# Head 0 of a hybrid trunk layer: recurrent input loaded and convolved during the input projection, loads from two queues, no barrier, an own place for the last modulation row

## The reference, cut to what matters

```python
sh1, sc1, g1, sh2, sc2, g2 = jnp.split(mod, 6, axis=-1)      # mod = silu(c) @ w_mod + b_mod
proj = h @ lp['w_in']
xr, gr, q, k, v, gates = jnp.split(proj, SPLITS, axis=-1)    # 1024, 1024, 1024, 1024, 1024, 4096 columns
xc = centred_conv(xr, lp['conv_w'], lp['conv_b'])            # 4 taps along the tokens
y, h_fin = rglru_bidir(xc, wr, br, wi, bi, lam, h0)          # r, i = sigmoid(block_diag(xc, w)); two scans
out_a = (y * jax.nn.gelu(gr)) @ lp['w_a_out']
q, k = apply_rope(q), apply_rope(k)                          # latent tokens only
o = diff_attn(q, [ctx_k, k], [ctx_v, v], lam)                # two softmax maps a head, 8 heads of 128 columns
out_b = rmsnorm(o) @ lp['w_b_out']
out = (sigmoid(ga) * out_a + sigmoid(gb) * out_b) @ lp['w_o']
```

## Time and profile before

| | us |
|---|---|
| median of 3 runs | 2991.76 |
| lowest and highest run | 2989.57, 2995.67 |
| profiled execution, span | 2987.8 |
| TensorE busy | 2856.4 |
| VectorE busy | 2190.0 |
| ScalarE busy | 1555.4 |
| GpSimd busy | 285.9 |

### The profile page before, as it was taken

One profiled execution on the slowest core, in us unless ns is written; L12 is line 12 of the kernel. 1 busy time (PEld: TensorE's weight loads), 2 busy tenths in 40 slices (PEclk: granted clock), 3 DMA queues, 4 the chain that ended last, 5 costly groups with the idle time before them and its releaser, 6 DMA issues.

```text
span 2987.8 us, 42700 instructions
## 1 busy us (share of the span) xinstructions
PE 2856.4 (96%) x15690; PEld 2306.2 (77%) x15690; DVE 2190.0 (73%) x1948; ACT 1555.4 (52%) x1510; POOL 285.9 (10%) x350
## 2 busy tenths in 40 slices
PE   7999999999899999999999995999999999999994
PEld 3589999998899999989998773666666666666662
DVE  7639688795677777763344467888888888888886
ACT  7721212224455555552232444777777777777774
POOL 1000000002111111100000000000000001101100
PEclk9999999999999999999999997999999999999997
DMA  9668677683333333354443655999999999999996
GB/s 378 243 210 257 203 251 238 212 267 100 105 118 118 118 118 118 118 185 139 119 134 130 243 207 218 357 387 390 377 396 382 388 385 385 377 380 381 391 385 239
DMA packets 292924, 757.58 MB, mean 254 GB/s; under 512 B 20329, under 2 KB 184721, under 8 KB 228193
## 3 DMA queue, kind: packets, MB, share of 16 engines
q1 hardware_dynamic: 266640, 638.47, 59.0%
q0 software_dynamic: 23664, 102.29, 10.6%
q10 hardware_dynamic: 2544, 15.82, 1.3%
HBM read 700.61 MB, written 55.89 MB: 253 GB/s over the span
## 4 chain that ended last, share of the span: by engine, by line
PE 79%; DVE 10%; issue 4%; DMA 4%; ACT 3%; DVEq 0%; SPq 0%; POOL 0%; ACTq 0%; POOLq 0%
PE ps L480 16%; PE ps L481 15%; PE ps L482 15%; PE ps L2039 7%; PE ps L2041 7%; PE ps L2040 7%; DVE mod_acc L1386 4%; PE ps L2175 2%; PE ps L2174 2%; PE ps L2176 2%; PE ps L1943 2%; PE ps L2102 1%; DMA raw<-in_w_mod 1%; DVE probs L1602 1%; DVE w_lo L435 1%
## 5 line engine op out<-in xcount | busy, mean ns | idle before, releaser
L413 DVE TENSOR_TENSOR we_lo<-raw,we_hi 128x2048 fp32r<-128x2048 f32 x384 | 876.4, 2290 | 137.2 <-ACT we_hi L408 136.8
L408 ACT ACTIVATE we_hi<-raw 128x2048 fp32r<-128x2048 f32 x384 | 736.8, 1919 | 285.0 <-PE ps L482 285.0
L2039 PE MATMUL ps<-hi,w_lo 128*128 128x320 f32 x2048 | 642.8, 314 | 9.1 <-DVE w_lo L384 4.8
L2041 PE MATMUL ps<-hi,w_hi 128*128 128x320 f32 x2048 | 633.9, 310 | 0.0
L2040 PE MATMUL ps<-lo,w_hi 128*128 128x320 f32 x2048 | 633.8, 309 | 0.0
L384 DVE TENSOR_TENSOR w_lo<-raw,w_hi 128x2048 fp32r<-128x2048 f32 (+1 forms) x120 | 272.7, 2273 | 211.0 <-ACT w_hi L374 205.8
L2039 PEld LDWEIGHTS ps<-hi,w_lo 128*128 128x128 f32 x2048 | 385.7, 188 | 26.4 <-issue 14.9
L481 PE MATMUL ps<-we_lo,xs_hi 128*80 128x512 f32 x1024 | 402.9, 393 | 0.0
L480 PE MATMUL ps<-we_hi,xs_lo 128*80 128x512 f32 x1024 | 402.2, 393 | 0.1
L482 PE MATMUL ps<-we_hi,xs_hi 128*80 128x512 f32 x1024 | 400.1, 391 | 0.0
L2040 PEld LDWEIGHTS ps<-lo,w_hi 128*128 128x128 f32 x2048 | 385.9, 188 | 0.2
(11 more groups left out here) (384 smaller groups left out, 3945.5 us busy)
## 6 DMA issues: line engine op xcount, KB each, us to landing
raw<-in_w_e_gate SPq DMA_DIRECT2D x128, 1024.0 KB, 7.2
raw<-in_w_e_up SPq DMA_DIRECT2D x128, 1024.0 KB, 8.2
raw<-in_w_e_down SPq DMA_DIRECT2D x128, 1024.0 KB, 12.1
raw<-in_w_in SPq DMA_DIRECT2D x144, 512.0 KB, 5.3
mod_raw<-in_w_mod SPq DMA_DIRECT2D x64, 1024.0 KB, 5.2
raw<-in_w_mod SPq DMA_DIRECT2D x64, 512.0 KB, 6.3
raw<-in_w_o SPq DMA_DIRECT2D x64, 512.0 KB, 4.7
d_proj<-stage POOLq DMA_DIRECT2D x32, 320.0 KB, 3.7
```

The source lines that it names most:

```text
L408: act.activation(we_hi[:, k % NEH, :], raw_slot(k), ACT.Copy).then_inc(hi_ready, 2)
L413: TTn(we_lo[:, k % NEH, :], raw_slot(k), we_hi[:, k % NEH, :].bitcast(F32), ALU.subtract).then_inc(lo_ready, 2)
L2039: pe.matmul(out, wl, hi[:, k, ms], start=(k % 16 == 0), stop=False)
L2041: last = pe.matmul(out, wh, hi[:, k, ms], start=False, stop=(k == KT - 1))
```

## The change

Head 0's part of the work is pulled ahead, and its barrier goes.

- GpSimd issues xr and the recurrent weights of head 0 behind the store of unit 26 (`load_recurrent`), k_past and k behind the issue of the store of unit 31, then q_in, gr and v once that store has landed.
- VectorE does `parameters(0)` and `conv(0)` behind the split of unit 30, `gates_lo(0)` behind `mod_low` of unit 31. ScalarE does `gates_hi(0)` behind its split in unit 31.
- The last modulation row gets a place of its own, `m_row3`, in raw slot 2, and its bias is loaded behind unit 30. `mod_row2` waits for the sum itself now, and so does TensorE ahead of `lru0` for the row.
- SyncE issues rope and the eight turned pieces of head 0, behind the fourth modulation sum and ahead of the gate unit 3.
- `change` is replaced by a bare addition to `phase`, without drain and without wait. VectorE waits for the stored modulation rows ahead of `take_T(0)`.
- Head 0 has no table of its own on TensorE: the loop runs over all eight, and `keys` moves from behind piece 1 to behind piece 2 in all of them. `k_loaded` counts 80 a head with 16 for head 0.
- Buffers are laid out anew: `sc` and `sel` behind `mod_raw`, `lru_w`, `xc` and `xr` where nothing of the projection lies.

```diff
-        sel = at("sel", [P, 2, 2], F32R, PLACED["ones2"] + 64)
-        mod_at = PLACED["ones2"] + 128
+        mod_at = PLACED["ones2"] + 64
+        A["sc"] = at("sc", [P, 32], F32, mod_at + NMOD * UB)
+        sel = at("sel", [P, 2, 2], F32R, mod_at + NMOD * UB + 128)
...
+        m_row3 = at("m_row3", [2, D], F32, raw_at + 2 * UB)
...
+                if u == 31:
+                    sp.wait_ge(S["mod_summed"], 4)
+                    sp.dma_start(C["rope"][:], a["rope"]).then_inc(S["rope_loaded"], 16)
+                    sp.wait_ge(S["in_stored"], 25 * 16)
+                    for turned, n in (("k_turn", 24), ("q_turn", 16)):
+                        for r in range(0, P, HD // 2):
+                            sp.dma_start(C[turned][r:r + HD // 2, :], ...).then_inc(S["turns0_loaded"], 16)
...
             for u in range(32):
                 wait(pool, "in_taken", 2 * (u + 1))
                 pool.dma_start(d_proj[u * P:(u + 1) * P, :], stage[:, u % 2, :]).then_inc(S["in_stored"], 16)
+                if u == 31:
+                    pool.wait_ge(S["mod_lo"], 8)
+                    load_past(0)
+                    load_rows(0, "k", 24, "k_loaded")
                 stored("in_stored", (u + 1) * 16, "stage_free")
+                if u == 26:
+                    pool.wait_ge(S["zero_stored"], TT * 16)
+                    load_recurrent(0)
+                if u == 30:
+                    pool.wait_ge(lo_ready, 2 * NRAW + 2 * (Q_IN * NRAW + 30 + 1))
+                    pool.dma_start(m_row3[:], a["b_mod"][0:1, 5 * D:6 * D].to_broadcast([2, D])
+                                   ).then_inc(S["b_loaded"], 16)
-                if u % 8 == 7:
+                if u % 8 == 7 and u < 31:
...
-            pool.wait_ge(S["zero_stored"], TT * 16)
-            change(pool, 2, False)
+            pool.sem_inc(phase, 1)
+            load_rows(0, "q_in", 16, "q_loaded")
+            load_rows(0, "gr", 8, "gr_loaded")
+            load_values(0)
+            wait(pool, "m_row_ready", 6)
+            pool.dma_start(d_mod[:, 5 * D:6 * D], m_row3[:]).then_inc(S["m_stored"], 16)
+            pool.wait_ge(S["m_stored"], 4 * 16)
...
             for u in range(32):
                 split_hi(act, Q_IN + u // 4, u % 4 + 1)
+                if u == 31:
+                    gates_hi(0)
...
-            change(act, 2)
+            act.sem_inc(phase, 1)
...
             def mod_row2(g):
+                dve.wait_ge(S["mod_summed"], g + 1)
                 dve.wait_ge(S["b_loaded"], (g + 1) * 16)
...
+                if u == 30:
+                    parameters(0)
+                    for step in range(4):
+                        conv(0, step)
                 if n == 7:
                     mod_low(g)
+                if u == 31:
+                    gates_lo(0)
             mod_row2(3)
-            change(dve, 2)
+            dve.sem_inc(phase, 1)
...
-                    dve.wait_ge(S[loaded], h * 80 + 80)
+                    dve.wait_ge(S[loaded], h * 80 + 16)
+                    dve.wait_ge(S["turns0_loaded"], 8 * 16)
...
+                    if qt == 0:
+                        dve.wait_ge(S["m_stored"], 4 * 16)
...
-            leave(pe)
+            pe.sem_inc(phase, 1)
...
                 def lru(d):
                     if d == 0:
+                        wait(pe, "m_row_ready", 6)
...
-            head(0, {5: "keys", 6: "lru0", 7: "lru1", 14: "s0", 21: "s1", 22: "t0", 24: "s2", 25: "t1", 27: "s3",
-                     29: "t2", 30: "s4", 31: "t3 t4 values mean"})
-            with pe.Fori(1, NH) as h:
-                head(h, {1: "keys", 3: "lru0", 4: "lru1", 10: "s0", 18: "s1", 19: "t0", 21: "s2", 22: "t1", 24: "s3",
+            with pe.Fori(0, NH) as h:
+                head(h, {2: "keys", 3: "lru0", 4: "lru1", 10: "s0", 18: "s1", 19: "t0", 21: "s2", 22: "t1", 24: "s3",
                          26: "t2", 27: "s4", 28: "t3", 30: "t4 values", 31: "mean"})
```

More of the change, by code:

```diff
@@ L186, in trunk @@
         m_row2 = at("m_row2", [2, D], F32, s0)
[L187 removed]
+        m_row3 = at("m_row3", [2, D], F32, raw_at + 2 * UB)
+        assert s0 + 15360 + 2 * UB <= PLACED["rows1"] and mod_at + NMOD * UB + 192 <= s_end
         v_stage = at("v_stage", [P, TT, 512], F32, s0)
@@ L538, in _ @@
                 mod_tiles(u // 8, u % 8)
+                if u == 31:
[4 more added lines that the diff above has]
+                        for r in range(0, P, HD // 2):
+                            sp.dma_start(C[turned][r:r + HD // 2, :],
+                                         d_proj[n * P + (r ^ (HD // 2)):n * P + (r ^ (HD // 2)) + HD // 2, 0:N_LAT]
+                                         ).then_inc(S["turns0_loaded"], 16)
                 c0 = (u + 4) * P if u < 28 else GATE_COL + (u - 28) * P
@@ L683, in _ @@
                     pool.dma_start(d_mod[:, (g + 2) * D:(g + 3) * D], m_row2[:]).then_inc(S["m_stored"], 16)
-            pool.wait_ge(S["zero_stored"], TT * 16)
-            change(pool, 2, False)
+            pool.sem_inc(phase, 1)
[5 more added lines that the diff above has]
+            pool.wait_ge(S["m_stored"], 4 * 16)
             def load_head(h):
[L689 to L692, removed]
+                load_recurrent(h)
                 turns = (("k", "k_turn", 24, "k_loaded"), ("q_in", "q_turn", 16, "q_loaded"))
                 for name, _, n, ready in turns:
[L695 to L699, removed]
+                    load_rows(h, name, n, ready)
+                load_past(h)
                 for _, turned, n, ready in turns:
@@ L703, in load_head @@
                                        d_proj[bass.ds((h + n) * P + (r ^ (HD // 2)), HD // 2), 0:N_LAT]).then_inc(S[ready], 16)
[L704 to L709, removed]
-                               ).then_inc(S["v_loaded"], 16)
+                load_rows(h, "gr", 8, "gr_loaded")
             def head(h, last):
@@ L1455, in gates_lo @@
                 TTn(lw_lo[:], C["lru_w"][:], lw_hi[:].bitcast(F32), ALU.subtract).then_inc(S["gates_lo"], 1)
-            parameters(0)
-            for step in range(4):
-                conv(0, step)
-            gates_lo(0)
+            for u in range(32):
+                g, n = u // 8, u % 8
+                split_lo(dve, Q_IN + u // 4, u % 4 + 1)
+                if n == 0 and g:
+                    mod_row2(g - 1)
+                for k in range(MOD_FROM[n], MOD_FROM[n] + MOD_TILES[n]):
+                    mod_tile(g, k)
+                if u == 30:
+                    parameters(0)
+                    for step in range(4):
+                        conv(0, step)
+                if n == 7:
+                    mod_low(g)
+                if u == 31:
+                    gates_lo(0)
+            mod_row2(3)
+            dve.sem_inc(phase, 1)
             def post_vectors():
```

62 lines of the change are left out of this document (32 added, 30 removed).

## The result

The changed kernel takes 2973.66 us (median of 4 runs, 2973.01 to 2975.28) against 2992.74 us of the kernel before (4 runs): ratio 0.9938, 95% interval 0.9926 to 0.9951. That is 19.1 us less; the forecast of 2972.7 was 1.0 us too low.

The account below looks back on a forecast made before the run. TensorE is busy 2856.4 of 2987.8 us, so time is won only where it idles or runs slowly. Gain 12.32 + 6.83 + 0.25 - 0.3 = 19.1 us; 2991.8 - 19.1 = 2972.7 us, range 2969 to 2981.

Parts of the forecast that it names:

- The loss of head 0: TensorE in head 0 against head 2: 12.37 us idle (0.05 in head 2) plus 6.83 us slow clock, 19.15 us.
- first stop: TensorE waits 3.82 us for k_past ahead of its transposition at 715.47, half clock behind it; gone with early loads.
- later stops: TensorE waits in head 0, one of 3.9 us for ScalarE's gate bank copy; the common table removes them.
- Its two causes: Head 0's stops: loads queued behind the last modulation row's barrier, and scores 3 placed ahead of a piece needing ScalarE's bank.
- Free places: Convolution, splits and copies fit idle time at the projection's end, price 0; keys land 3.6 us before TensorE needs them.
- The rotation: Head 0's tables and turned rows land by 709.5; VectorE copies keys by 713.5, no later than in head 2.
- Barrier and drains: The 0.36 us issue gap ahead of head 0 lies before a loop entry and stays; 0.3 us given back.
- Not given back later: Behind head 0 every engine works in step with TensorE, so what is won there is not given back.
- Rival D: The early recurrent loads hurt the input projection by 2 us: 2974.7 us; chance 0.05.
- A: Head 0: k lands after 706.25 because two queues share DMA engines; 6.3 us lost, 2979.0 us; chance 0.09.
- B: Head 0's small loads and VectorE's wait keep the later stops; only the first stop goes, 2985.2 us; chance 0.05.
- C: Keys one piece later make VectorE wait and TensorE stop in all eight heads: 50 us, 3023 us; chance 0.04.

Follow-up runs that it names:

- e3: Changed kernel with the old TensorE table for head 0, loads still early: 2985.87 us, ratio 0.9981; head 0 83.8 us.
- e4: Kernel before with only the table changed, all eight heads in one loop, keys behind piece 2: 2984.85 us, ratio 0.9974; head 0 84.9 us.
- e9: Changed kernel with the keys behind piece 1 instead of piece 2 in all heads: 2970.17 us, ratio 0.9928; head 0 72.9 us.
- e7: Changed kernel with rope and the eight turned pieces issued from GpSimd's queue instead of SyncE's: 2973.14 us, ratio 0.9941; head 0 73.0 us.
- e8: Changed kernel with the barrier and its drains kept behind the last modulation row: 2973.75 us, ratio 0.9945; head 0 73.8 us.
- e5: Changed kernel with xr and recurrent weights loaded behind the last store, convolution and splits behind the last modulation row: 2975.68 us, ratio 0.9945; head 0 76.7 us.
- e6: Changed kernel with k_past and k issued last, behind q_in, gr and v: 2981.90 us, ratio 0.9967; head 0 80.9 us.

## Why the prediction was right

**The loss of head 0** was read as 19.15 us plus 0.25 in head 1. By the marks of the table head 0 gave 92.3 - 73.0 = 19.3 us, heads 1 to 7 0.3 to 0.9. Both parts, idle time and slow clock, went whole, and a comparison of an odd head with its repeated fellows was enough to size them. One reading was wrong: the 6.83 us of slow clock don't all come from the stretch behind the first stop. The stretches of 715 to 725 in the kernel before have 0.50 and 0.89, by their busy time an estimate of 2.8 us; those of 770 to 775 and 785 to 790, behind the later stops, have 0.73 and 0.66, by the same estimate another 2. The rest isn't accounted for. The sum didn't need that split.

**Its two causes** were named rightly: e3 and e4 each take one away. The first stop was put down to k_past alone, and TensorE waited there for the turned rows of k as well (see e4). I priced the loads at 6.3 us and the later stops at 12 to 13; the loads alone gave 8.5, the return of the old table cost 10.8. The mechanism was right and the split was 2 us off. That the two prices depend on each other, by 3.4 us, stands nowhere in the prediction.

**Free places.** Convolution and the copies hid where I put them. The keys had room: TensorE reached them at 703.94, 5.3 us into the head (I had 5.4), and e9 took them a piece earlier without a stop. The new wait for the modulation row was met by 5 us: 698.85 + 2.28 = 701.1 against 705.9.

**The rotation: this step failed.** I had all nine loads landed within 4.4 us of the last issue, and VectorE at the copy of the keys no later than in head 2. The turned rows took 5.2 to 6.6 us to land, in a crowd of rope, q_in, gr, v and gate weights. VectorE reached that copy at 713.80, 15.0 us behind the end of the sum. I had 713.5 - 700.5 = 13.0 at the latest, and head 2 has 13.4. It cost nothing, as the scores start only 8 us later, at 721.91; e7 shows the same.

**Barrier and drains: a term that was wrong by 0.3 us.** I gave back 0.3 us for an issue gap that would stay. It went, and e8 puts it at 0.6 to 0.8 us with the drains.

**"Not given back later": this step failed too, by 2 us.** The branch projections are 1.8 us longer with the loop over all heads, and the projection itself took 0.5 us longer than before, its wait for w_lo 4.3 us instead of 3.8. Rival D had asked for up to 2 us from the early recurrent loads. But e5, without these, has 470.4 us as well, so they are not the cause; which part of the change is was not tried. By stages the change is worth 19.3 + 0.6 - 1.8 - 0.5 = 17.6 us, which lies within the intervals of both comparisons (0.9947 is 16 us).

**Luck in the number.** The medians differ by 19.1 and 20.5 us, not by 17.6. The stage ahead of the projection, which the prediction doesn't name, was 1.7 us shorter on average in the changed kernel's two profiles than in the two of the kernel before. Over all profiles it took 227.9 to 231.8 us, and no run ties it to the change. So the 2.3 us that the prediction missed behind head 0 and in the projection were nearly made up by a difference that it didn't foresee: that head 0 gave 19.3 us is skill, that the time came out within 1.0 us is in part luck.

**The rivals.** A, late keys, was real as a mechanism: made by the edit of e6, a stop of 6.0 us cost 7.9 in head 0, where I had priced a stop of 3.82 at 6.3. In the changed kernel it didn't come: k was there before TensorE. B fell with the changed kernel, which has these small loads still and no stop, and e3 shows that the later stops hang on the table alone. C fell: heads 1 to 7 did not lengthen, and e9 shows no effect of the move.

## What to carry to other kernels

Where one pass of a repeated stage is longer than its fellows with the same work, the difference is the price of its odd surroundings; split it into idle time and slow clock, and look for both an order of its own and data of its own that comes late. The barrier itself cost 0.8 us here, and the work queued behind it most of 8.5: look at what is queued behind a barrier, and move the loads that the next stage reads first ahead of it, into idle time of the stage before. Two edits that meet at one wait are not to be priced apart: here they gave 8.5 and 7.4 us alone and 19.3 together. And a stage that comes out as forecast doesn't vouch for the others: compare all of them, also those ahead of the change.

## What the runs showed of the hardware

- A stop of TensorE of 6.0 us was followed by a granted clock of 0.53 and 0.79 over the next 10 us and cost 7.9 us in all (e6); the two stops of 1.9 and 1.3 us in e5 left it at 1.00 in every stretch of 5 us from 700 to 715. But in one profile (e6) a stop of 1.79 us in the projection was followed by 0.66 over 5 us, with 25 matmuls in them, and in another (e3) one of 1.83 us at the same place by 1.00, with 36.
- The four pieces of q_turn, 64 KB each, landed 2.3 us after issue on GpSimd's queue in the kernel before, 4.0 on the same queue in e7, and 6.6 from SyncE's queue beside GpSimd's in the changed kernel. Head 0 was 73.0 us in both of the latter; whether the crowd alone made the difference was not tried.
- The same code gave an output projection of 250.5 or 253.6 us from one execution to the next, and over all profiles 247.3 to 255.3 us. A median needs several runs to see 2 us through that.
